# Expert blocks of 64 + 32 rows: the branch's rows over four column groups, units of three blocks, three buffers for each kind of weights

## What is computed

```python
def routed_experts(xt, expert_id, weights, w_gate, w_up, w_down):
    ...
    padded = (counts + MOE_BLOCK - 1) // MOE_BLOCK * MOE_BLOCK
    ...
    def expert_block(args):
        xs, e = args
        hid = jax.nn.silu(xs @ w_gate[e]) * (xs @ w_up[e])
        return hid @ w_down[e]
    yb = lax.map(expert_block, (xb, block_expert)).reshape(n_slots, D)
    contrib = yb[slot] * w_sorted[:, None].astype(yb.dtype)
    return jax.ops.segment_sum(contrib, tok_sorted, num_segments=T)
```

## Time and profile before

| what | value |
|---|---|
| median of 3 runs | 3381.0 us (3378.68 to 3386.77) |
| time of the profiled execution | 3375.32 us |
| its span, first to last instruction | 3373.6 us |
| TensorE matmul busy | 3079.4 us, 91% |
| TensorE weight load busy | 1627.6 us, 48% |
| VectorE, ScalarE, GpSimd busy | 37%, 26%, 17% |
| mean granted TensorE clock | 0.952 of full speed |
| bytes moved | 613.06 MB, mean 182 GB/s |

### The profile page before, as it was taken

The page is one execution under the profiler, slowest core; times in us unless marked ns, Lnnn a source line. Parts: engine busy times, 40 slices in busy tenths (PEclk is TensorE's granted clock), DMA queues, the critical chain, the costliest instruction groups (busy, mean ns, idle before and its releaser), DMA issues. The chain is left out here.

```text
span 3373.6 us, 41645 instructions
## 1 busy us (share of the span) xinstructions
PE 3079.4 (91%) x14759; PEld 1627.6 (48%) x14760; DVE 1246.2 (37%) x2998; ACT 887.3 (26%) x1754; POOL 572.8 (17%) x1019
## 2 busy tenths in 40 slices
PE   8969999698969999998899999999999969988886
PEld 6536544485434333443566666666544434333332
DVE  5867754573442122222433332233312231222224
ACT  1034333142221111111345544445501110111111
POOL 0000010461101122121211111111100001122223
PEclk9979999798979999999899999999999979999998
DMA  8910011233179899985411011110041087899975
GB/s 331 353 42 1 1 32 44 64 82 104 56 298 363 337 380 413 400 351 200 170 38 38 4 35 38 38 38 1 0 145 37 32 344 305 354 426 424 412 314 220
DMA packets 182218, 613.06 MB, mean 182 GB/s; under 512 B 55193, under 2 KB 106132, under 8 KB 149046
## 3 DMA queue, kind: packets, MB, share of 16 engines
q1 hardware_dynamic: 150998, 566.46, 43.2%
q0 software_dynamic: 22080, 42.01, 3.2%
q10 hardware_dynamic: 8992, 2.62, 0.3%
HBM read 592.59 MB, written 53.00 MB: 191 GB/s over the span
## 5 line engine op out<-in xcount | busy, mean ns | idle before, releaser
L1969 PE MATMUL ret_pqkv<-ret_w,hT_mix 128*128 128x512 f32 x1024 | 452.4, 595 | 2.2 <-PEq L2709 2.2
L2542 PE MATMUL f0e_pgu<-f0w_gu,f0e_xT 128*64 128x512 f32 x1568 | 345.4, 596 | 8.5 <-issue 4.7
L1831 PE MATMUL mo_py<-mo_w,mixT 128*128 128x512 f32 x768 | 335.1, 597 | 4.7 <-DMA mo_w<-in_hy_w_out_dram 2.5
L2542 PE MATMUL f1e_pgu<-f1w_gu,f1e_xT 128*64 128x512 f32 x1344 | 296.8, 597 | 7.5 <-issue 3.8
L1969 PEld LDWEIGHTS ret_pqkv<-ret_w,hT_mix 128*128 128x128 f32 x1024 | 190.5, 191 | 218.2 <-issue 218.2
L1831 PEld LDWEIGHTS mo_py<-mo_w,mixT 128*128 128x128 f32 x768 | 146.0, 192 | 186.6 <-issue 178.7
L2542 PEld LDWEIGHTS f0e_pgu<-f0w_gu,f0e_xT 128*64 128x64 f32 x1568 | 124.5, 138 | 224.0 <-issue 224.0
L1977 PE MATMUL ret_pgate<-ret_w,hT_mix 128*128 128x256 f32 x1024 | 231.6, 379 | 0.0
L2561 PE MATMUL f1e_pd<-f1w_d,f1e_hidT 128*64 128x512 f32 x672 | 167.1, 648 | 43.4 <-DMA f1w_d<-in_moe_w_down_dram 41.5
L1977 PEld LDWEIGHTS ret_pgate<-ret_w,hT_mix 128*128 128x128 f32 x1024 | 189.6, 190 | 23.6 <-issue 0.5
L2542 PEld LDWEIGHTS f1e_pgu<-f1w_gu,f1e_xT 128*64 128x64 f32 x1344 | 103.6, 138 | 195.3 <-issue 195.2
(11 more groups left out here) (565 smaller groups left out, 4485.3 us busy)
## 6 DMA issues: line engine op xcount, KB each, us to landing
f0w_gu<-in_moe_w_gate_dram SPq DMA_DIRECT2D x32, 2048.0 KB, 10.9
f0w_gu<-in_moe_w_up_dram SPq DMA_DIRECT2D x32, 2048.0 KB, 16.5
f0w_d<-in_moe_w_down_dram SPq DMA_DIRECT2D x64, 1024.0 KB, 13.1
f1w_gu<-in_moe_w_gate_dram SPq DMA_DIRECT2D x32, 2048.0 KB, 15.4
f1w_gu<-in_moe_w_up_dram SPq DMA_DIRECT2D x32, 2048.0 KB, 25.7
f1w_d<-in_moe_w_down_dram SPq DMA_DIRECT2D x64, 1024.0 KB, 14.2
mixT<-in_ada_w_dram SPq DMA_DIRECT2D x80, 512.0 KB, 5.7
ret_w<-in_ret_w_in_dram SPq DMA_DIRECT2D x16, 1024.0 KB, 10.0
```

The source lines that it names most:

```text
L1831: mm = pe.matmul(py[t % 3][:, half * 512:(half + 1) * 512], mixT[:, kk, t * P:(t + 1) * P], ws[:, kk, half * 512:(half + 1) * 512], start= ...
L1969: mm = pe.matmul(p_qkv[s % 2][:, :], g.hT[:, kk, t * P:(t + 1) * P], w[h % 2][:, kk, 0:512], start=(kk == 0), stop=(kk == KD - 1))
L2542: mm = pe.matmul(pgu[s][half * HALF:(half + 1) * HALF, :], xT[u % 2][:, kk, s * HALF:(s + 1) * HALF], ew.gu[u][:, :, kk, half * FH:(half + ...
```

## The change

A block now has CAP = 96 rows: LOW = 64 rows, computed as before, and REST = 32 rows behind the branch. With 32 rows the stationary operand is 32 columns wide, and the output columns are cut in four quarters, each on a group of 32 array columns: `gate_up_rest` has 8 slices x 4 groups = 32 matmuls of 256 moving columns, `down_rest` 4 x 4 = 16 of 256. The hidden rows of the rest are transposed by four small matmuls with the identity, and their results are written as four quarters of 1 KB. Rows past the 96th of an expert go to blocks from 32 on.

Groups of blocks (units) have 3 blocks instead of 4. The number of blocks is a multiple of 3: 33 in layer 0, the last one empty (its expert is number 31), and 33 in layer 1, the last one with the 4 pairs of expert 6 that don't fit its first block. Every block loads the 6.29 MB of its expert.

There are three buffers of everything: `gu` (before four), `d` (before two), `xg`, `xT`, `y` (before two). The rows that `mix_out` leaves turned (`hT`) are freed before `route`, so that all six weight buffers are there from its start, and `first_loads` issues gu and d of three blocks. SyncE's order is gu, d of one block, then gu, d of the next; gu of block b+3 waits for the gates of b, d of b+3 for the downs of b.

In `route`, the shifts and masks by 128 become multiplications by 1/96 with rounding; a second copy of the layer's gate vector is made for quarters.

```diff
-NBLK = PAIRS // P + NE
-QUAD = 4
+LOW, REST = 64, 32
+CAP = LOW + REST
+UNIT = 3
+NBLK = (PAIRS // CAP + NE) // UNIT * UNIT + UNIT
...
-            ts(usf[:, i:i + 1], cum[0:1, NE - 1:NE], 1.0 / QUAD, NE / QUAD + 0.375 - i, ALU.mult, ALU.add)
+            ts(usf[:, i:i + 1], cum[0:1, NE - 1:NE], 1.0 / UNIT, (NE + 1) / UNIT - i, ALU.mult, ALU.add)
...
     def first_loads(self, sp):
-        self.load_gu(sp, 0, 0)
-        self.load_gu(sp, 1, 1)
-        self.load_d(sp, 0, 0)
-        self.load_gu(sp, 2, 2)
+        for u in range(UNIT):
+            self.load_gu(sp, u, u)
+            self.load_d(sp, u, u)
...
-        idx = [sb(f"idx{u}", [P, 1], I32) for u in range(2)]
+        idx = [sb(f"idx{u}", [P, 1], I32) for u in range(UNIT)]
...
-        xT = [sb(f"xT{u}", [P, KD, P]) for u in range(2)]
-        hs = [sb(f"hs{s}", [P, FH]) for s in range(2)]
-        hid = [sb(f"hid{s}", [P, FH]) for s in range(2)]
+        xT = [sb(f"xT{u}", [P, KD, CAP]) for u in range(UNIT)]
+        hs = [sb("hs0", [P, FH]), sb("hs1", [P, FQ])]
+        hid = [sb("hid0", [P, FH]), sb("hid1", [P, FQ])]
...
-                for u in range(QUAD):
-                    load_gu(m, u, now[u])
-                    if u < QUAD - 1:
-                        load_d(m - 1, u + 1, old[u])
-                    else:
-                        load_d(m, 0, now[0])
...
+                for u in range(UNIT):
+                    sp.wait_ge(S["gu_a"], m * UNIT + (u - UNIT + 1))
+                    sp.wait_ge(S["gu_b"], m * UNIT + (u - UNIT + 1))
+                    ew.load_gu(sp, u, now[u])
+                    sp.wait_ge(S["down_a"], m * UNIT + (u - UNIT + 1))
+                    sp.wait_ge(S["down_b"], m * UNIT + (u - UNIT + 1))
+                    ew.load_d(sp, u, now[u])
...
+            def gate_up_rest(u):
+                for kk in range(KD):
+                    for c in range(2):
+                        for h in range(2):
+                            q, f = 2 * c + h, h * FH + c * FQ
+                            mm = pe.matmul(pgu[1][q * REST:(q + 1) * REST, 0:2 * FQ], xT[u][:, kk, LOW:CAP],
+                                           ew.gu[u][:, :, kk, f:f + FQ], start=(kk == 0),
+                                           stop=(kk == KD - 1), skip_group_check=True)
+                return mm
...
-                for s in range(2):
-                    for j in range(2):
-                        mm = pe.transpose(ph[:, (2 * s + j) * P:(2 * s + j + 1) * P], hid[s][:, j:FH:2],
-                                          g.ident[:, :])
+                for j in range(2):
+                    pe.transpose(ph[:, j * P:(j + 1) * P], hid[0][:, j:FH:2], g.ident[:, :])
+                for j in range(2):
+                    for c in range(2):
+                        part = slice(c * 64, (c + 1) * 64)
+                        mm = pe.matmul(ph[part, 4 * LOW + j * 2 * REST:4 * LOW + (j + 1) * 2 * REST],
+                                       hid[1][part, j:FQ:2], g.ident[part, part], start=True, stop=True,
+                                       skip_group_check=True)
...
+            def down_rest(u):
+                for k in range(KF):
+                    for q in range(4):
+                        mm = pe.matmul(pd[1][q * REST:(q + 1) * REST, 0:DQ], hidT_rest[:, k % 2, k // 2, :],
+                                       ew.d[u][:, k, q * DQ:(q + 1) * DQ], start=(k == 0), stop=(k == KF - 1),
+                                       skip_group_check=True)
+                return mm
...
+            router = Router(g, logits0, "f0l", 0)
             turned_rows(g, ffn0, "ffn0")
-            router = Router(g, ffn0, "f0l", 0)
             mix_out(g, "mo0", o.mixT, KD, io["hy_w_out"][0], x, x1, 0, router)
-        ahead = moe(g, "f0", x1, x2, 0, ffn0, router, retention_ahead)
+        ffn0.close()
+        ahead = moe(g, "f0", x1, x2, 0, logits0, router, retention_ahead)
```

More of the change, by code:

```diff
@@ L2242, in _ @@
                                stop=True, skip_group_check=True)
+            for c in range(4):
+                mm = pe.matmul(pgate4[c * REST:(c + 1) * REST, 0:D // 4], g.ones[:, 0:REST], diag[:, 2 * c:2 * c + 2, :],
+                               start=True, stop=True, skip_group_check=True)
             mm.then_inc(S["gated"], 1)
@@ new lines, in scatter @@
+                for s, (rows, parts) in enumerate(((halves, 2), (quarters, 4))):
+                    pool.indirect_dma_start(out=rows, out_offset=bass.IndirectOffsetOnAxis(ap=didx[u][:, s:s + 1], axis=0),
+                                            in_=y[u][s][:, :], in_offset=None, bounds_check=parts * PAIRS - 1,
+                                            oob_is_err=False).then_inc(slots["stored"][u], 16)
+            with pool.Fori(1, units_used(pool)) as m:
+                for u in range(UNIT):
```

352 lines of the change are left out of this document (166 added, 186 removed).

## The result

The changed kernel took **3355.0 us** (median of 4, 3352.7 to 3356.1), the kernel before in the same series 3381.6. The ratio is **0.9919, 95% interval 0.9902 to 0.9936**: 27 us faster, where 58 were forecast. The time lies inside the stated range of 3292 to 3385. The profiled execution has a span of 3354.4 us (before: 3373.6).

The account below looks back on a forecast made before the run. TensorE bound layer 0's experts and transfers mostly layer 1's; after the change transfers would bind. Layer 0 -42.5, layer 1 -16.9, route +1 sum to -58 us from the 3381.0 median: 3323 us, range 3292 to 3385.

Parts of the forecast that it names:

- the order starves nothing once the transfers are the limit. Only the start has holes: SyncE's load order: over 25 us of loads stay outstanding in steady state, so waiting for downs before gu costs nothing there.
- The rest at 3.75 and 1.95 us: Second part of a full block on TensorE, four column groups side by side: 3.75 us in gates, 1.95 in downs.
- Rivals A and B: Second part: A, only two groups at once, 3414 us, chance 0.12; B, four hindering each other, 3336 to 3361, chance 0.14.
- The allowance of 0.3 and 0.2 us: TensorE's second part: margin in the gates' and downs' figures for switching between 64 and 32 columns.
- Transfers at 416 GB/s in steady state: Weight and row transfers of the experts: full queue at 416 GB/s, 539.5 us per layer, 16.35 per block.
- Rival C: Experts' transfers run slower, at 410 or 400 GB/s: 8 or 22 us more per layer, 3339 to 3367, chance 0.11.
- Holes of 17 and 27.6 us at the start: Transfers of the first blocks: idle gaps while loads wait for buffers, 17 us in layer 0, 27.6 in layer 1.
- Layer 1, last landing plus 12.8 us: End of layer 1's experts: last load lands 3270.5, tail 12.8, end 3283.3 against 3300.2, so -16.9 us.
- Layer 0, last landing plus 14.7 us: End of layer 0's experts: last load lands 1508.4, tail 14.7, end 1523.1 against 1565.6, so -42.5 us.
- Eleven turns at the price of before: TensorE's loop turns in layer 0: 11 instead of 8, with no term of their own in the forecast sum.
- The 33rd block at 16.35 us of transfers: Extra block in both layers, 33 instead of 32: 16.35 us of transfers, 12.1 on TensorE, included in the layer's sum.
- Rival D, TensorE's clock: TensorE idling for gu drops to half clock: blocks without second part cost 24 us, 20 blocks +160 us, chance 0.03.

## Why the prediction came out as it did

The prices of the parts were right within a few tenths of a us. Two steps failed. The first is "the order starves nothing once the transfers are the limit. Only the start has holes": with gu ahead of w_down in SyncE's order each layer is 15 us shorter. The second is a term that stood at nothing, the turns of the loop on TensorE: with one flag read there instead of four the layers are 7.5 and 12 us shorter. With both mended the kernel takes 3315 us, where 3323 were forecast.

- **The rest at 3.75 and 1.95 us: right**, measured 3.66 and 1.94. Rivals A and B fall. A loss at each change of width doesn't: 3.59 us pass from the rest's start to the next transpose, where 64 matmuls of 256 columns, four at once, are 8 x 0.43 = 3.43, and the first part of the downs takes 3.58 where it took 3.48. The allowance of 0.3 and 0.2 us covered it. By the Trainium skill (TensorEngine Tiling, Key Properties) a change of tiling mode drains the engine; at most 0.16 us of that can be in this row. The estimate of 4.3 us from the Trainium skill's three groups (TensorE: Matmul & The Clock Gate, Measured speedup vs the span model) was too high: the row has 3.66.
- **Transposes 1.7: slightly low**, 1.88, 6 us of TensorE over 33 blocks.
- **Transfers at 416 GB/s in steady state: right.** 415 GB/s in 1200 to 1500 and 414 in 2900 to 3200, share 1.00. Rival C falls.
- **Holes of 17 and 27.6 us at the start: right in sum.** 20 in layer 0; 21 + 7 = 28 in layer 1's first two stretches (0.79 and 0.93). But I took them as given by the change, where 8 us in each layer are the order's (1000 to 1200 and 2700 to 2900 us), and with the turn mended too only 3 and 9 are left.
- **Layer 1, last landing plus 12.8 us: wrong.** The last gu landed 3257.95 - 2676.40 = 581.5 us after the first load; the forecast's line puts it at 568.6 - 5 = 563.6, 18 us earlier. Of these, 8 are the half-empty engines: in the three stretches from 3245 to 3260 they moved (274 + 166 + 151) x 5 us = 3.0 MB, of 6.2 that they could. That isn't the order's doing. With order and turn mended the last gu lands at 3215.93, and the stretches ahead of it lack 8 us as well:

```profile
3190.00:3195.00 5.00, 5.00 (x32) 1.87 (x28) 0.00 (x0) 0.55 (x2) 0.00 (x0) 1.00 0.85 346
3195.00:3200.00 5.00, 4.85 (x32) 2.09 (x28) 2.35 (x8) 1.40 (x4) 0.00 (x0) 1.00 0.50 210
3200.00:3205.00 5.00, 4.77 (x22) 1.63 (x24) 0.99 (x2) 0.00 (x0) 2.35 (x4) 1.00 0.88 346
3205.00:3210.00 5.00, 5.00 (x34) 2.51 (x32) 1.32 (x4) 1.76 (x6) 1.06 (x1) 1.00 0.77 313
3210.00:3215.00 5.00, 2.78 (x14) 0.72 (x10) 2.02 (x6) 0.19 (x1) 0.18 (x1) 1.00 0.44 184
```

So a thin tail belongs to the end of a layer here, and the forecast had none; why the engines run half empty with loads still out isn't shown. Another 4 us: when the last gu landed 0.5 MB were left, not the 2.1 MB of the forecast. The remaining 6 are bytes that came late before: 540 us after the first load 389 GB/s x 540 us = 210.1 MB had passed, where the line has 416 x (540 - 1.5 - 27.6) = 212.6. The order bears on this: with order alone it is 398 x 540 = 214.9 MB, and the last gu lands after 568.3 us. Behind the landing came 21.0 us instead of 17.8, since the gates ran at the low clock (9.99 us).
- **Layer 0, last landing plus 14.7 us: wrong in form.** From the landing of gu of block 30 (1486.3) TensorE never waited again: blocks 30 and 31 are full, and 53.7 us of its own work stood behind. By the pace of the forecast's line that landing would have been 553.0 - 2 x 16.35 = 520.3 us after the first load and the end at 574; it was 537.7. I read off only when the last bytes come, not where TensorE's own chain takes over. By chance both ways give nearly the same end; the 19 us that layer 0 missed are this landing, 17 us late, and the order and the next point say what held TensorE, and so the loads, back.
- **Eleven turns at the price of before: wrong.** The sum had no term for them; the earlier trace rows had 4.7 us of "issue" in layer 0 that I let pass. The gap is 2.5 to 2.9 us behind a full block, five times in layer 0 (0.5 to 0.6 behind the others), and behind four of the five the gates lose another 1.5 to 1.7 at the low clock. That it takes both the reads and the dense rest is shown; the reason, which no row shows directly, is most likely that the small matmuls (32 in 1.9 us at the turn) leave TensorE's sequencer no lead when it stops to read four flags. TensorE's line from the first gates took 1540.0 - 989.3 = 550.7 us where 504 were forecast (990.1 to 1494): 14.6 us are these gaps, 245.9 - 33 x 7.04 = 13.6 slow gates (7 behind the gaps, 3.5 behind waits for gu, and 2.5 in the first two gates, which the forecast had in its 8), 15.9 waits for gu, 6 the transposes. The waits for gu are the order's for the most part: with order alone 6.9 are left.
- **The 33rd block at 16.35 us of transfers**: not tested alone in layer 1; its loads have no price in layer 0, where they end ahead of TensorE's own line. TensorE's 12 us for it weren't tested.
- **Rival D, TensorE's clock, at 0.03: not half clock for the block, but not nothing.** The granted clock was 0.93 in 2900 to 3200, and most gates behind a wait for gu of over 2 us took 8.5 to 10 us. In a stage bound by transfers this mostly fills idle time; in the tail it doesn't.

With order and turn mended layer 0 takes 572.5 us, and 572.7 were forecast. That is no confirmation: of the 17 us of holes at the start 3 are left, and from 1480 on, where the forecast still had the engines full, they stand at 0.66 and 0.36 while TensorE works to the end without a pause. Two misses of opposite sign meet.

## What to carry to other kernels

When a queue issues loads for several kinds of buffers in one order, write down for each load which wait stands ahead of it, its own or that of another kind; here the second sort cost holes at the stage's start, and its middle moved fewer bytes though the share read full. Work out a stage's end from both chains, the last bytes and the other engine's remaining work. When matmuls are made smaller so that more run side by side, look at everything that the sequencer does between them, such as reads, branches and waits: what long matmuls hid may then stand open. Where a change adds code to a loop, look at the instruction queue of the profile too. A long wait for a load in a stage bound by transfers isn't a price: ask what the stage's time would be without it.
